# A hybrid decoder step: expert weights loaded two items at a time, activations stored in groups of four

## What is computed

```python
def block(tb):
    qv = (tb @ wq).reshape(n, PEER_HEADS, 2, PEER_HALF)
    s = jnp.einsum('thcd,hckd->thck', qv, sub_keys)
    s_top, i_top = lax.top_k(s, PEER_TOPK)
    ...
    best, pos = lax.top_k(cand, PEER_TOPK)
    idx = jnp.take_along_axis(cand_idx, pos, axis=-1)
    g = jax.nn.softmax(best, axis=-1)
    act = jax.nn.gelu(jnp.einsum('td,thkd->thk', tb, expert_u[idx]))
    return jnp.einsum('thk,thkd->td', g * act, expert_v[idx])
```

## Time and profile before

| | |
|---|---|
| median of three executions | 1911.04 us |
| the profiled execution, its own time | 1913.67 us |
| its span on the core | 1911.9 us |
| PE busy | 1802.4 us, 94% |
| DVE / ACT / POOL busy | 1487.0 / 858.2 / 518.3 us |
| bytes moved by DMA | 462.67 MB |
| plain DMA queue (q1) / gather queue (q0) | 293.00 / 167.79 MB |

### The profile page before, as it was taken

One profiled execution on the slowest core, in us unless ns is written; L12 is line 12 of the kernel. 1 busy time (PEld: TensorE's weight loads), 2 busy tenths in 40 slices (PEclk: granted clock), 3 DMA queues, 4 the chain that ended last, 5 costly groups with the idle time before them and its releaser, 6 DMA issues.

```text
span 1911.9 us, 29712 instructions
## 1 busy us (share of the span) xinstructions
PE 1802.4 (94%) x11394; PEld 1738.7 (91%) x11394; DVE 1487.0 (78%) x2660; ACT 858.2 (45%) x1272; POOL 518.3 (27%) x415
## 2 busy tenths in 40 slices
PE   5999989997999999999999999699999999999996
PEld 4999987787999999999999999699999999988995
DVE  5736597567568778999999999588888788787777
ACT  4557673223333333437777777333233233232263
POOL 2200120000000002244444444444444444434300
PEclk9999999999999999999999999899999999999998
DMA  3222333114334446789999999999999999998611
GB/s 131 78 69 78 110 99 116 68 56 165 125 125 133 154 172 213 242 282 348 365 374 364 351 359 360 387 387 376 374 365 385 382 383 382 349 342 319 209 56 47
DMA packets 163915, 462.67 MB, mean 242 GB/s; under 512 B 16640, under 2 KB 76736, under 8 KB 161216
## 3 DMA queue, kind: packets, MB, share of 16 engines
q1 hardware_dynamic: 117696, 293.00, 42.4%
q0 software_dynamic: 46080, 167.79, 23.4%
HBM read 405.46 MB, written 55.27 MB: 241 GB/s over the span
## 4 chain that ended last, share of the span: by engine, by line
PE 69%; DVE 14%; DMA 11%; ACT 3%; issue 2%; SPq 0%; DVEq 0%; ACTq 0%
PE PS L448 11%; DMA Rw<-vn 9%; PE PS L1469 8%; PE PS L1470 8%; PE PS L1471 8%; PE PS L1482 5%; PE PS L1483 5%; PE PS L1484 5%; PE PS L1458 5%; PE PS L1535 4%; PE PS L2041 2%; DVE Hl L1845 2%; ACT Rh L164 1%; DVE Rl L169 1%; DVE ug L1853 1%
## 5 line engine op out<-in xcount | busy, mean ns | idle before, releaser
L169 DVE TENSOR_TENSOR Rl<-Rw,Rh 128x1024 fp32r<-128x1024 f32 x272 | 332.3, 1222 | 180.4 <-ACT Rh L164 177.1
L164 ACT CAST Rh<-Rw 128x1024 fp32r<-128x1024 f32 x272 | 284.2, 1045 | 393.6 <-PE PS L1484 342.1
L1424 POOL DMA_INDIRECT ug<-un,idxU x160 | 240.1, 1501 | 577.3 <-DVE dots L1853 351.1
L1482 PE MATMUL PS<-Hh,Rh 128*128 128x384 f32 x1024 | 353.5, 345 | 40.0 <-DVE Hl L1845 40.0
L1469 PE MATMUL PS<-Xh,Rh 128*128 128x384 f32 x1016 | 351.2, 346 | 3.8 <-DVE Rl L169 2.8
L1483 PE MATMUL PS<-Hl,Rh 128*128 128x384 f32 x1024 | 350.6, 342 | 0.0
L1484 PE MATMUL PS<-Hh,Rl 128*128 128x384 f32 x1024 | 350.2, 342 | 0.0
L1470 PE MATMUL PS<-Xl,Rh 128*128 128x384 f32 x1016 | 342.3, 337 | 0.0
L1471 PE MATMUL PS<-Xh,Rl 128*128 128x384 f32 x1016 | 341.3, 336 | 0.0
L1424 POOL DMA_INDIRECT ug<-vn,idxU x160 | 234.4, 1465 | 287.0 <-DVE yacc L1858 222.8
L1482 PEld LDWEIGHTS PS<-Hh,Rh 128*128 128x128 f32 x1024 | 196.0, 191 | 49.5 <-issue 49.3
(11 more groups left out here) (430 smaller groups left out, 3139.6 us busy)
## 6 DMA issues: line engine op xcount, KB each, us to landing
Rw<-uw SPq DMA_DIRECT2D x144, 512.0 KB, 5.0
Rw<-vn SPq DMA_DIRECT2D x128, 512.0 KB, 7.8
Wr<-wm SPq DMA_DIRECT2D x51, 512.0 KB, 3.3
acts<-Ab SPq DMA_DIRECT2D x128, 192.0 KB, 5.4
gates<-stg SPq DMA_DIRECT2D x12, 2048.0 KB, 9.4
Gq<-gates SPq DMA_DIRECT2D x16, 1536.0 KB, 13.1
Aq<-acts SPq DMA_DIRECT2D x32, 768.0 KB, 9.2
L<-acsd SPq DMA_DIRECT2D x4, 1024.0 KB, 7.8
```

What stands on the lines that cost most here:

```text
L164: a.copy(self.Rh[:, q, :], self.Rw[:, q, :]).then_inc(self.S("rhi"), 1)
L169: v.tensor_tensor(self.Rl[:, q, :], self.Rw[:, q, :], self.Rh[:, q, :].bitcast(F32), ALU.subtract).then_inc(self.S("rlo"), 1)
L1424: p.indirect_dma_start(out=ug[:, r % 4, :], out_offset=None, in_=un if r < IDC else vn, in_offset=bass.IndirectOffsetOnAxis(ap=idxU[:, r % ...
L1482: pe.matmul(out, Rh[:, q, w], hh, start=(g == 0), stop=False)
```

## The change

`layout` on the host packs items 2p and 2p + 1 side by side, so that each partition's two rows of 4 KB lie together in DRAM (`ew`, [136, 128, 2, 1024]). `Ring.load(p)` fetches both with one DMA of 1 MB, 8 KB per partition, into two of the four slots. It waits until item 2p - 3 has been split, and both items wait for the same DMA. SP issues it at odd m only. `acts` is laid out as [32, 128, 4, 384]: `store_act` writes the same 1.5 KB per partition, now 6 KB apart, and `load_a` reads 6 KB per partition in one piece where it read four of 1.5 KB. The matmuls, `hi`, `lo` and the gathers are as before (the gathers read their own copies of the tables).

```diff
@@ class Ring @@
-    def load(self, sp, m):
-        q = m % 4
-        if m >= 4:
-            sp.wait_ge(self.S("rhi"), m - 3)
-            sp.wait_ge(self.S("rlo"), m - 3)
-        src = self.uw[m, :, :, :].rearrange("p k j -> p (k j)") if m < NIT else self.vn[(m - NIT) * P:(m - NIT + 1) * P, :]
-        sp.dma_start(self.Rw[:, q, :], src).then_inc(self.S("rw%d" % q), 16)
+    def load(self, sp, p):
+        if p >= 2:
+            sp.wait_ge(self.S("rhi"), 2 * p - 2)
+            sp.wait_ge(self.S("rlo"), 2 * p - 2)
+        q = p % 2
+        sp.dma_start(self.Rw[:, 2 * q:2 * q + 2, :], self.ew[p, :, :, :]).then_inc(self.S("rw%d" % q), 16)
 
     def hi(self, a, m):
         q = m % 4
-        a.wait_ge(self.S("rw%d" % q), 16 * (m // 4 + 1))
+        a.wait_ge(self.S("rw%d" % (q // 2)), 16 * (m // 4 + 1))
@@ mixer, sync @@
-        for m in range(4):
-            ring.load(sp, m)
+        for p in range(2):
+            ring.load(sp, p)
@@ experts @@
-    acts = nc.dram_tensor("acts", [PK, P, DT], F32, kind="Internal").ap()
+    acts = nc.dram_tensor("acts", [PK // 4, P, 4, DT], F32, kind="Internal").ap()
@@ experts, sync @@
-            sp.dma_start(acts[u, :, :], Ab[:, u % 4, :]).then_inc(S("as%d" % (u % 4)), 16)
+            sp.dma_start(acts[u // 4, :, u % 4, :], Ab[:, u % 4, :]).then_inc(S("as%d" % (u % 4)), 16)
...
-            sp.dma_start(Aq[:, i % 3, :, :], acts[4 * i:4 * i + 4, :, :].rearrange("i p t -> p i t")
-                         ).then_inc(S("aq%d" % (i % 3)), 16)
+            sp.dma_start(Aq[:, i % 3, :, :], acts[i, :, :, :]).then_inc(S("aq%d" % (i % 3)), 16)
...
-            if m < NALL:
-                ring.load(sp, m)
+            if m < NALL and m % 2 == 1:
+                ring.load(sp, m // 2)
@@ layout @@
-    uw = np.empty((NIT, P, ND, P), np.float32)
-    uw[QITEM] = tiles(g["peer_wq"][0])
-    uw[UITEM] = u.reshape(PK, PK, ND, P).transpose(0, 3, 2, 1)
-    d["uw"] = uw
+    ew = np.empty((NIT + PK, P, D), np.float32)
+    ew[QITEM] = tiles(g["peer_wq"][0]).reshape(2 * PH, P, D)
+    ew[UITEM] = u.reshape(PK, PK, ND, P).transpose(0, 3, 2, 1).reshape(PK, P, D)
+    ew[NIT:] = g["peer_v"][0].reshape(PK, PK, D)
+    d["ew"] = np.ascontiguousarray(ew.reshape(-1, 2, P, D).transpose(0, 2, 1, 3))
```

More of the change, by code:

```diff
@@ L143, with __init__ @@
 class Ring:
-    def __init__(self, nc, sh, uw, vn, start):
-        self.S, self.uw, self.vn = sh.sem, uw, vn
+    def __init__(self, nc, sh, ew, start):
+        self.S, self.ew = sh.sem, ew
         (self.Rw, self.Rh, self.Rl), self.end = plan(
             nc, start, ("Rw", [P, 4, D], F32), ("Rh", [P, 4, D], F32R), ("Rl", [P, 4, D], F32R))
-    def load(self, sp, m):
-        q = m % 4
-        if m >= 4:
-            sp.wait_ge(self.S("rhi"), m - 3)
-            sp.wait_ge(self.S("rlo"), m - 3)
-        src = self.uw[m, :, :, :].rearrange("p k j -> p (k j)") if m < NIT else self.vn[(m - NIT) * P:(m - NIT + 1) * P, :]
-        sp.dma_start(self.Rw[:, q, :], src).then_inc(self.S("rw%d" % q), 16)
+    def load(self, sp, p):
[4 more added lines that the diff above has]
+        sp.dma_start(self.Rw[:, 2 * q:2 * q + 2, :], self.ew[p, :, :, :]).then_inc(self.S("rw%d" % q), 16)
     def hi(self, a, m):
         q = m % 4
-        a.wait_ge(self.S("rw%d" % q), 16 * (m // 4 + 1))
+        a.wait_ge(self.S("rw%d" % (q // 2)), 16 * (m // 4 + 1))
         if m >= 4:
@@ L2242, in closing, with build @@
     return (early_sync, early_scalar, early_vector), (sync, pool, tensor, scalar, vector)
-def build(nc, x, wm, par, head, w_rg, w_ig, conv_in, s0, lru0, keys, uw, vn, un, pT, w_plg, w_plp, y, ssd_p, ssd_s, conv_o, lru_o):
+def build(nc, x, wm, par, head, w_rg, w_ig, conv_in, s0, lru0, keys, ew, vn, un, pT, w_plg, w_plp, y, ssd_p, ssd_s, conv_o, lru_o):
     with ExitStack() as ctx:
         sh = Shared(nc, ctx)
-        ring = Ring(nc, sh, uw, vn, sh.free + RING_AT)
+        ring = Ring(nc, sh, ew, sh.free + RING_AT)
         early, last = closing(nc, sh, pT, w_plg, w_plp, y)
```

## The result

The changed kernel takes 1952.17 us, the median of four executions (1948.74 to 1958.37), where the kernel before had 1912.65 us in four (1910.48 to 1920.91). The ratio is 1.0205 with a 95% interval of 1.0179 to 1.0231: some 2% slower, on the side that was forecast, and 18 us above the predicted 1934. That is 2 us above the 1922 to 1950 that the forecast gave for itself, and inside the whole range of 1890 to 1962. The profiled execution of after took 1951.64 us, its span is 1949.9 us (1911.9 before), its mean clock 0.974 (0.981).

The account below looks back on a forecast made before the run. PE was taken to bound the U stage and in V to idle for `Hl`, held by one late weight load; 14.0 + 7.0 - 0.2 + 2 = 22.8 us on 1913.67, less 2.6 to the median, gave 1934 us, range 1890 to 1962.

Parts of the forecast that it names:

- Steps 1 and 3: V rounds with gates: pair ahead of gates adds 1.20 us; item 4t + 10 coming with 4t + 11 adds 1.20 us.
- Step 3: V rounds with gates: item 4t + 10 comes with 4t + 11, +1.20 us; its issue 3.2 us later costs nothing.
- Step 4: V rounds with gates: engines alternate queues by packet, so longer pieces push one gather behind item 4t + 10, -1.30 us.
- the V term: V stage: net +0.93 us in each of 15 rounds with gates, 14.0 us, plus 7.0 us for the clock.
- Step 5, rounds without gates: V stage: the pair stands behind 1.92 us of activations and lands well inside the round; nothing lost.
- Step 5, the clock: V stage: lost PE clock adds half as much again to the 14.0 us, 7.0 us.
- Step 5, the start: Start of the V stage: activations of group 0 land 0.2 us earlier.
- Step 6: U stage: casts 1 to 2 us late at six places behind gates stores, mostly hidden; 2 us, range 0 to 18.
- Packet turns make it faster: V stage: more than 14 gather packets a round pushed behind weights, `Hl` waits shrink; 1890 us, cap 1875; chance 0.13.
- Fewer transfers: V stage: each of 64 saved loads had an unhidden fixed part, so `Hl` waits go altogether; 1873 us; chance 0.03.
- Gathers starve: V stage: weights' larger share delays gathers, holding DVE, `lo` and `Hl`; 27 us more, about 1960 us; chance 0.10.
- U stage: U stage: pairs behind gates stores hold ACT's one-hots and PE's gate matmuls; up to 16 us more, 1950; chance 0.05.

Follow-up runs that it names:

- e10: Against e2: one 1 MB DMA per two items from the two old tensors, 4 KB pieces, activations grouped; 1957.26 us, ratio 1.0248 to the kernel before.
- e2: Kernel before with only the activations grouped (6 KB pieces), weights still loaded item by item; 1904.89 us, ratio 0.9976 to the kernel before.
- e4: Changed kernel with two 512 KB DMAs, a semaphore each, at the pair's place and condition; 1946.76 us, ratio 1.0196 to the kernel before.
- e3: Changed kernel with each pair's tiles apart in DRAM, so the 1 MB DMA reads 4 KB pieces; 1957.25 us, ratio 1.0249 to the kernel before.
- e6: Changed kernel with pairs in the U stage only, single loads from the paired layout in V; 1925.07 us, ratio 1.0087 to the kernel before.
- e5: Changed kernel with pairs in the V stage only, single loads from the paired layout in U; 1951.5 us, ratio 1.0221 to the kernel before.
- e12: e11 with gates laid out to load 12 KB per partition and store in 1 KB pieces; 1910.42 us, ratio 0.9986 to the kernel before.
- e9: e2 with all weights in one DRAM tensor, each tile contiguous, single loads, no pairs; 1909.44 us, ratio 1.0003 to the kernel before.
- e1: Changed kernel with activations stored and read as before, in 1.5 KB pieces, so pairs only; 1958.67 us, ratio 1.0268 to the kernel before.
- e11: Kernel before with grouped activations and each gates load issued two items later; 1903.18 us, ratio 0.9973 to the kernel before.

## Why the prediction was right, and where it was not

**The sign and the chain: right.** PE's wait for `Hl` grew, through the load behind the activations, in the rounds with gates above all. +23.5 us in the V stage stand against +21.0.

**Steps 1 and 3, the pair ahead of the gates and the second half: right in kind, somewhat too large.** They were priced at 1.20 us each for a round, 2.40 x 15 x 1.5 = 54 us with the clock. The clean measure of both is e10 against e2: 46.7 us in V, or 42.7 if e10's profiled execution is shifted to its median. The parts are known less well. e4 lets go of the halves one by one and gets 8.7 us back in V; as it also gives up the 8 KB pieces, whose gain was 7 to 11 us in V (590.3 against e3's 597.7 and e10's 601.1), the second half by itself is some 16 to 20 us, and more if e4's rows 8 KB apart cost it something. The later request for the even items is the 13 to 19 us between e6 and e4; 8.9 of it fall in the fifteen intervals with gates.

**Step 3, "costs nothing, because the activations ahead of it are not through by then": the cover held.** The issue is 2.4 to 3.8 us behind `Aq`, as forecast, and in after the activations land 9.7 to 14.3 us behind theirs in the rounds with gates. So what the later request costs in those rounds more likely comes through step 1, by item 4t + 8, than through the issue of item 4t + 10; this is read from the landings, and no run moves the one without the other.

**Step 4, the packet turns: right in sign, too large.** It was counted at -1.30 us a round, with clock -29 us in all. e3 against after measures it at -5 (-7.4 in V), and in the waits at 4.3 us less for `Hl` and 11.3 more for gathers. Some of what the weights gain, DVE gives back in front of the same `Hl`: the chain passes through gathers in four of the rounds with gates. The count of turns also left out the gates themselves. Their 1.5 MB in pieces of 1 KB stand in the queue ahead of the activations, and the gathers go beside them. In the kernel before, 1399 to 1401 us, while the gates issued at 1393.58 were under way:

```profile
q0 software_dynamic: 134, 0.46, 57.8%
q1 hardware_dynamic: 255, 0.26, 40.5%
```

In after the gates issued at 1422.20 land after 13.7 us, at 1435.9, and the three gathers behind the `Hl` are issued from 1427.94 to 1431.70. Most of the 24 gather packets per engine can go before a single packet of activations does, with the change as without it, so few are left to be pushed behind item 4t + 10. That is an argument from these rows; no run tests it. These rows also show 255 packets of the plain queue beside 134 of the gathers, so the turns are not one for one with pieces of 1 KB. And the packet of the profile is one piece, where that of the Trainium skill (DMA: Bandwidth & Descriptors, "Queues, rings and completion order") is a bundle of typically 9 to 17 descriptors: the 58 and 66 packets agree with turns between the queues, and do not show how much goes in one turn.

So the V term came out near by luck. Step by step in the V stages of the profiled executions: the activations gave -12.4 us (before to e2; forecast -0.17 x 15 x 1.5 = -3.8), the pairing +46.7 (e2 to e10; forecast +54), the longer pieces -10.8 (e10 to after, which also changes the tensor; forecast -29). Shifted by how before and e10 lie beside their medians these are -8.6, +42.7 and -6.3. A gain overrated by 18 to 23 us stands against a cost overrated by 7 to 11 and another gain underrated by 5 to 9. Each part is known to some 5 us.

**Step 5, rounds without gates, "Nothing": wrong.** These went from 17.85 to 18.40 us each, 7.7 us over the fourteen; the V stage as a whole grew by 23.5. From e6 to e4 alone they grow by 4.7 us together. One of them is in the chain of after: the pair issued at 1559.89, in a round without gates, lands after 13.65 us. The activations ahead of the pair are through after 4.0 to 7.5 us there, so the cover is thinner.

**Step 5, the clock: half.** The waits behind the first grew by 19.2 us, the V stage by 23.5, so 4.3 us came on top where 7.0 were forecast (0.22 instead of 0.5 for each us of idle PE). How much of the 4.3 is the clock is known only roughly: it was granted at 0.97 from 1234 to 1805 us before and at 0.96 from 1248 to 1842 after, with PE busy for 543.2 and 546.7 us.

**Step 5, the start: wrong in sign.** "-0.2" was +2.9. The activations of group 0 took 15.10 us to land against 12.30. Why is not settled.

**Step 6, the U stage: the term that was mis-sized.** It was put at 2 us, in a range to 18, and measured 8.9: 4.8 at the turn and 4.1 from there. The working looked for late casts at the places with a pair right behind a store (counted as six; it is seven of the twelve). Late casts there are, 47.0 us of waits for weights in eleven times, and most of that is hidden, as stated. What was missed is the turn: at 860 to 882 us PE was busy 22.00 of 22.00 us and is busy 17.42 now. There ACT's copies of `ijg` come once and everything of the gates follows from them, so nothing hides a cast that is 4.49 us late. The kernels without pairs vary there by 4.0 us (404.7 to 408.7, leaving out e5), so the 4.8 us is uncertain by about as much; e12, which has no pairs, has a weight load in its chain at the turn too (8.60 us, from 858.69). The other 4.1 us are in part the last store of gates, 12.31 against 9.80 us, for which the first loads of `Gq` and `Aq` wait; why it lands later no run told.

**The rivals.** *Packet turns make it faster*: the mechanism exists (e3), at 5 us. *Fewer transfers*: no run shows a gain from half as many DMAs; e10 has half of e2's weight loads, with all else alike, and is 52 us slower. The Trainium skill's rule of at least 1 MiB per DMA (DMA: Bandwidth & Descriptors, "Measured") would have it the other way; that rule is measured there on DMAs issued from GpSimd, and the traces here don't agree with it for loads that SP issues and that are queued behind each other, with the engines at work 95 to 102% of the time. *Gathers starve*: the gathers' waits tripled, and taking that away (e3) makes the kernel slower. *U stage*: it came besides the forecast, at over half of its price (8.9 us, 11.8 with the start, for 16).

**The signs.** `Hl` 64.5 us in 17 times, for 54 in 16; the landing in the chain 12.2 to 14.9 us in rounds with gates, for 14 to 16; the issue 2.4 to 3.8 us behind `Aq`, for 3 to 4; `Aq` to `Aq` 20.1 and 18.4 on average, for 18 to 19 and 17; DVE's waits for gathers 19.5 us, just below the 20 named; the gathers in the chain land in 10.5 to 12.3 us, more than the 8.5 to 9.5 forecast for all, of which the profile of after has no median; 770 to 1205 us has PE 4.5 us less busy, more than the 3 allowed; and the U stage got longer, one of the three signs named for being wrong.

**What stays open.** Why the last store of gates and the first activations land 2.5 and 2.8 us later; what the later request costs with rows that are not 8 KB apart (e4 was not made on the old tensors), and how it divides between items 4t + 8 and 4t + 10; and how much of the turn's 4.8 us is scatter.

## What to carry to other kernels

A bigger DMA is not free where a ring of few slots feeds an engine: with four slots, loading two at a time makes every even item start one slot later and every even item wait for its neighbour, which together cost 2.7% here (e10 against e2), and no run shows a gain from the halved number of loads. Before making a load larger, look at what stands ahead of it in its queue and at who waits for the first half: moving one unrelated 1.5 MB load two places back in the queue was worth 31 us with pairs and 6.5 us without. And price a late load at the one place where a stage turns over, not only at the places that repeat.

## What the runs showed of the hardware

- Rows of 4 KB that lie 8 KB apart seem slower to live with than contiguous ones: e5's U stage, single items in the old order, is 9.5 us longer from `rstd_f` to the first load of `Aq` than e9's (768.5 against 759.0), and DVE's waits for gathers from 462 to 1236 us are 34.3 us in 23 times against 9.9 in 12. e6's V stage is 7.5 us longer than e9's (568.2 against 560.7). These are differences between single executions, e5's 7.3 us above its median: the waits are well apart, the lengths hardly.
- Pieces of 8 KB in place of 4 KB, the same bytes in the same DMA, moved 11.3 us of waiting onto the gathers of the other queue (e3 against after), beside activations in 6 KB pieces. With activations in 1.5 KB pieces the waits for gathers were 3.6 us (e1), with 8 KB pieces of weights as they were.
- A 2 MB store written in pieces of 1 KB instead of 16 KB made the gates stage 3.2 us longer (e12 against e11, one execution each), and reading it back in pieces of 12 KB instead of 1 KB showed no gain: ACT's waits for weights fell from 16.7 to 9.7 us and DVE's for gathers rose from 8.1 to 17.6.
